# A causal depthwise convolution of 31 taps on VectorE: two alternating sums, with ScalarE making the first taps and all of the small group's products

## The reference

```python
h = xn @ w_in
a, b, q, k, v, ga, gb = jnp.split(h, SPLITS, axis=-1)
glu = a * jax.nn.sigmoid(b)
...
def conv_branch(glu_hist, w_dw, b_dw, conv_ln_g, conv_ln_b, w_conv_out, b_conv_out):
    y = lax.conv_general_dilated(glu_hist, w_dw[:, None, :], window_strides=(1,), padding='VALID',
                                 dimension_numbers=('NWC', 'WIO', 'NWC'),
                                 feature_group_count=D_CONV) + b_dw
    y = jax.nn.silu(layernorm(y, conv_ln_g, conv_ln_b))
    return y @ w_conv_out + b_conv_out
```

## Time and profile before

| what | value |
|---|---|
| median of 3 runs (lowest, highest) | 1535.66 us (1534.71, 1536.74) |
| profiled execution, its own time | 1535.57 us |
| its span, first to last instruction | 1532.7 us |
| mean granted TensorE clock | 0.942 of full speed |
| busy over the span: PE, DVE, ACT, POOL | 86%, 74%, 41%, 18% |
| prompt taps, line 1108 | 240 instructions, 307.7 us busy |
| sample taps, line 1111 | 240 instructions, 66.6 us busy |

### The profile page before, as it was taken

How to read it: one execution, slowest core, us unless ns; L and a number is a source line. 1 busy time by engine, 2 the same in 40 slices (tenths; PEclk the granted TensorE clock), 3 DMA queues, 4 the chain that set the end, 5 groups by cost and what they waited for, 6 DMA issues and landing times. The chain is left out here.

```text
span 1532.7 us, 25464 instructions
## 1 busy us (share of the span) xinstructions
PE 1312.5 (86%) x8761; PEld 780.9 (51%) x8761; DVE 1140.4 (74%) x1553; ACT 631.9 (41%) x903; POOL 276.6 (18%) x276
## 2 busy tenths in 40 slices
PE   2589999976999998997978987888992999888885
PEld 2246666665666664664645554554552555443442
DVE  5437878886599999999998564543655899787783
ACT  5325565654211111111103262332311788767772
POOL 0027001000000000000000000000024476532333
PEclk9999999987799999998988999999995999999997
DMA  6520000022112221221222005427566889999962
GB/s 234 143 56 9 0 0 0 0 104 66 35 43 78 73 60 50 63 64 62 56 60 71 15 30 185 170 86 282 175 245 215 296 319 364 348 320 333 340 231 32
DMA packets 51055, 203.50 MB, mean 133 GB/s; under 512 B 14464, under 2 KB 15552, under 8 KB 38400
## 3 DMA queue, kind: packets, MB, share of 16 engines
q1 hardware_dynamic: 32032, 156.92, 28.1%
q0 software_dynamic: 16656, 36.84, 9.1%
q10 hardware_dynamic: 2304, 8.95, 1.9%
HBM read 180.92 MB, written 39.72 MB: 144 GB/s over the span
## 5 line engine op out<-in xcount | busy, mean ns | idle before, releaser
L1108 DVE SCALAR_TENSOR_TENSOR big<-c_region,c_taps,big 128x1024 f32 (+1 forms) x240 | 307.7, 1282 | 0.0
L72 PE MATMUL c_psb<-xnT,w_taken 128*128 128x364 f16 x456 | 146.4, 321 | 2.3 <-DVE f_w_l L1003 2.3
L73 PE MATMUL c_psb<-xnT,w_taken 128*128 128x364 f16 x456 | 146.2, 321 | 0.0
L74 PE MATMUL c_psb<-xnT,f_w_l 128*128 128x364 f16 x456 | 146.1, 320 | 0.0
L72 PE MATMUL c_psa<-xnT,w_taken 128*128 128x364 f16 x312 | 100.9, 323 | 17.3 <-DVE c_gate_b L1009 17.3
L72 PE MATMUL o_psH<-e_gu,big 128*128 128x512 f16 x256 | 100.9, 394 | 1.6 <-issue 1.5
L73 PE MATMUL o_psH<-e_gu,big 128*128 128x512 f16 x256 | 101.5, 397 | 0.0
L74 PE MATMUL o_psH<-e_gu,big 128*128 128x512 f16 x256 | 101.3, 396 | 0.0
L73 PE MATMUL c_psa<-xnT,w_taken 128*128 128x364 f16 x312 | 100.6, 323 | 0.0
L74 PE MATMUL c_psa<-xnT,f_w_l 128*128 128x364 f16 x312 | 100.6, 322 | 0.0
L2089 DVE SCALAR_TENSOR_TENSOR e_gu<-e_gu 128x2048 f16<-128x2048 f32 x34 | 77.8, 2290 | 19.7 <-ACT e_gu L1861 19.7
(11 more groups left out here) (338 smaller groups left out, 3382.1 us busy)
## 6 DMA issues: line engine op xcount, KB each, us to landing
e_gu<-w_gu SPq DMA_DIRECT2D x34, 1024.0 KB, 25.5
w_taken<-w_feat SPq DMA_DIRECT2D x48, 512.0 KB, 5.3
e_d<-w_dn SPq DMA_DIRECT2D x17, 1024.0 KB
xnT<-w_gu SPq DMA_DIRECT2D x14, 1024.0 KB, 35.9
big<-w_gu SPq DMA_DIRECT2D x14, 1024.0 KB, 33.1
m_gates<-gates POOLq DMA_DIRECT2D x8, 1092.0 KB, 5.8
xnT<-w_dn SPq DMA_DIRECT2D x7, 1024.0 KB
big<-w_dn SPq DMA_DIRECT2D x7, 1024.0 KB
```

The costliest lines, as they stand in the source:

```text
L72: pe.matmul(out, stat[0], mov[0], start=start, stop=False)
L73: pe.matmul(out, stat[0], mov[1], start=False, stop=False)
L74: return pe.matmul(out, stat[1], mov[0], start=False, stop=stop)
L1108: dve.scalar_tensor_tensor(y_p, glu[:, p, j:j + SEQ], tap, y_p, op0=ALU.mult, op1=ALU.add).then_inc(tap_done, 1)
```

## The change

`conv` keeps two sums for the prompt. Even taps add to `y`, odd ones to a new row `y_odd`, both rows of 1,024 columns of float32. Tap 0 with the bias and tap 1 are now made by ScalarE (`first_taps`), VectorE does taps 2 to 30 and adds the two rows at the end. For the sample group ScalarE makes all 31 products (`sample_taps`), 31 instructions of 64 columns, into `prods`, laid out as 31 blocks of 64 columns; VectorE adds them in one `tensor_reduce` whose inner axis steps 64 floats (256 bytes) from product to product. `y_odd` and `prods` lie in the area `caT`, which the first chunk's sample attention uses earlier and the layer norm later. Each tap now waits for the tap before the last one. The two inner calls of `low` move from after taps 11 and 20 to after taps 12 and 22 (19 and 27 in the first chunk), and `sample_norm` and `sample_out` of the first chunk move from after taps 5 and 11 to after 13 and 20.

```diff
+        y_odd = room32[:, 0:SEQ]
+        prods = room32[:, SEQ:SEQ + TAPS * TS].rearrange("p (j n) -> p j n", j=TAPS)
...
-        NTAP = 2 * TAPS
+        NTAP = TAPS
+        even_done, odd_done, prod_done, taps_go = sem("c_even"), sem("c_odd"), sem("c_prod"), sem("c_taps_go")
...
+            def first_taps(k, p):
+                act.wait_ge(glu_done, 2 * k + 1)
+                act.wait_ge(even_done, k)
+                act.sem_inc(taps_go, 1)
+                act.activation(row(y, k)[:, 0:SEQ], glu[:, p, 0:SEQ], ACT.Identity,
+                               scale=taps[:, ds(k, 1), 0:1].rearrange("p a b -> p (a b)"),
+                               bias=vecs[:, 0, ds(k, 1)]).then_inc(even_done, 1)
+                act.wait_ge(tap_done, NTAP * k)
+                act.sem_inc(taps_go, 1)
+                act.activation(y_odd, glu[:, p, 1:1 + SEQ], ACT.Copy,
+                               scale=taps[:, ds(k, 1), 1:2].rearrange("p a b -> p (a b)")).then_inc(odd_done, 1)
+
+            def sample_taps(k, p):
+                act.wait_ge(glu_done, 2 * k + 2)
+                act.sem_inc(taps_go, 1)
+                seqs = glu[:, p, HIST + SEQ:].rearrange("p (b n) -> p b n", b=NSEQ)
+                for j in range(TAPS):
+                    out = prods[:, j].rearrange("p (b i) -> p b i", b=NSEQ)
+                    tap = taps[:, ds(k, 1), j:j + 1].rearrange("p a b -> p (a b)")
+                    if j == 0:
+                        act.activation(out, seqs[:, :, 0:DSEQ], ACT.Identity, scale=tap,
+                                       bias=vecs[:, 0, ds(k, 1)]).then_inc(prod_done, 1)
+                    else:
+                        act.activation(out, seqs[:, :, j:j + DSEQ], ACT.Copy, scale=tap).then_inc(prod_done, 1)
...
                 cut(4 * k + 4, 0)
+                first_taps(k, p)
                 cut(4 * k + 5, 1)
...
                 gate_a_leaves(k)
                 cut(4 * k + 6, 2)
+                sample_taps(k, p)
...
                 dve.wait_ge(glu_done, 2 * k + 2)
+                dve.wait_ge(even_done, k + 1)
+                dve.wait_ge(odd_done, k + 1)
+                for j in range(2, TAPS):
                     tap = taps[:, ds(k, 1), j:j + 1].rearrange("p a b -> p (a b)")
-                    dve.wait_ge(tap_done, NTAP * k + 2 * j - 1)
-                    dve.scalar_tensor_tensor(y_p, glu[:, p, j:j + SEQ], tap, y_p, op0=ALU.mult,
+                    y_j = y_odd if j % 2 else y_p
+                    if j > 3:
+                        dve.wait_ge(tap_done, NTAP * k + j - 3)
+                    dve.scalar_tensor_tensor(y_j, glu[:, p, j:j + SEQ], tap, y_j, op0=ALU.mult,
                                              op1=ALU.add).then_inc(tap_done, 1)
...
+                dve.wait_ge(prod_done, TAPS * k + TAPS)
+                dve.tensor_reduce(y_s, prods.rearrange("p j n -> p n j"), AX.X, ALU.add).then_inc(tap_done, 1)
+                dve.wait_ge(tap_done, NTAP * k + TAPS - 2)
+                dve.tensor_tensor(y_p, y_p, y_odd, ALU.add).then_inc(tap_done, 1)
```

More of the change, by code:

```diff
@@ L928, in chunk @@
                     sample_new_probs()
+                    act.wait_ge(taps_ld, 16)
+                    act.wait_ge(vec_ld, 16)
                 cut(4 * k + 4, 0)
+                first_taps(k, p)
                 cut(4 * k + 5, 1)
@@ L1098, in conv @@
                 y_p = row(y, k)[:, 0:SEQ]
-                y_s = row(y, k)[:, SEQ:T].rearrange("p (b i) -> p b i", b=NSEQ)
+                y_s = row(y, k)[:, SEQ:T]
                 dve.wait_ge(glu_done, 2 * k + 2)
[L1101 to L1104, removed]
@@ L1105, in conv @@
-                for j in range(1, TAPS):
+                dve.wait_ge(even_done, k + 1)
+                dve.wait_ge(odd_done, k + 1)
+                for j in range(2, TAPS):
                     tap = taps[:, ds(k, 1), j:j + 1].rearrange("p a b -> p (a b)")
-                    dve.wait_ge(tap_done, NTAP * k + 2 * j - 1)
-                    dve.scalar_tensor_tensor(y_p, glu[:, p, j:j + SEQ], tap, y_p, op0=ALU.mult,
+                    y_j = y_odd if j % 2 else y_p
+                    if j > 3:
+                        dve.wait_ge(tap_done, NTAP * k + j - 3)
+                    dve.scalar_tensor_tensor(y_j, glu[:, p, j:j + SEQ], tap, y_j, op0=ALU.mult,
@@ L1109, in conv @@
                                              op1=ALU.add).then_inc(tap_done, 1)
[L1110 to L1113, removed]
+                    if first and j == 13:
                         sample_norm()
-                    if first and j == 11:
+                    if j == (19 if first else 12):
+                        low(4 * k + 6, 2)
@@ L1116, in conv @@
+                    if first and j == 20:
                         sample_out()
-                    if j == 11:
-                        low(4 * k + 6, 2)
                     if j == 18 and p == 1:
                         gated(u)
-                    if j == 20:
+                    if j == (27 if first else 22):
                         low(4 * k + 7, 3)
+                dve.wait_ge(prod_done, TAPS * k + TAPS)
+                dve.tensor_reduce(y_s, prods.rearrange("p j n -> p n j"), AX.X, ALU.add).then_inc(tap_done, 1)
```

## The result

| | kernel before | changed kernel |
|---|---|---|
| median (lowest to highest) | 1535.6 us (1534.7 to 1536.7) | 1518.4 us (1513.4 to 1521.5) |
| the profiled execution: time, span | 1535.6, 1532.7 us | 1521.5, 1519.0 us |
| ratio, 95% interval | | 0.9882 (0.9867 to 0.9897) |

The change takes 17 us off, 1.2%. Lines from 850 on have other numbers in the changed kernel: `glu` is L1048, `low` L1035, `gated` L1041, `cut` L856.

A forecast was written before the change was run, and what follows sets the result against it. VectorE's queue was taken to bound the kernel from chunk 1's start to the last tap. Gains of 9.6 us in the loop, 0.6 in chunk 1 and 5.4 at the turns sum to 15.6: 1520 us, range 1509 to 1531 (about 0.8).

The forecast's parts named there:

- VectorE sets the end, and what it saves from chunk 1 on comes off the total: From chunk 1's start to the last tap, VectorE's queue alone sets the end; seven chunks count, chunk 0's saving is lost.
- 29 long taps at 1.21 us: VectorE's remaining long taps in each chunk's convolution start 1.21 us apart, 35.1 us in all.
- The alternation itself gains nothing: Two sums bring no gain by themselves, since each long tap already had a short one between it and its predecessor.
- The reduce 3.6 us: VectorE's addition of the sample's products per chunk: 1,984 floats at 1.75 ns over 150 ns, 3.5 us after overlap.
- both bounds: Limits for the reduce: 2.2 us at the adjacent-element rate, 5.8 us at line 1991's whole duration per element.
- Rival 2: The reduce costs as with adjacent elements, 2.2 instead of 3.6 us, 9.8 us more gained: 1510 us; chance 0.11.
- Rivals 3 and 4: Dearer reduce: 2.1 to 2.9 ns per element, 1525 to 1535 us, chance 0.15; or beyond that, over 1539 us, 0.06.
- The new stall: VectorE waits 2.4 us per chunk before its second `low`, because ScalarE's second `cut` stands behind `first_taps`.
- The loop's turn: VectorE's gap from branch to next step falls from 2.9 to 0.2 us with the shorter body, twice: 5.4 us gained.
- ScalarE's products are free: ScalarE's 31 products, about 8 us per chunk, delay nobody; VectorE asks for them 35 us later.
- rival 5: ScalarE's small products take 1 us each and hold up `gate_b_leaves` by 15 us: about 1536 us; chance 0.03.
- `gated` 27.7 us after `glu`: In a chunk on VectorE, `gated` starts 27.7 us after `glu` instead of 31.3, so TensorE's stalls shrink.

## Why the prediction was right

Forecast 1520 us, measured 1518.4; forecast 15.6 us less in the stage, measured 17.3.

- **VectorE sets the end, and what it saves from chunk 1 on comes off the total.** Right. The 17.3 us of the stage reach the layer norm and the whole stretch to the experts' start as 16.5 us less (the 0.9 us between being chunk 1's later start), and the median fell by 17.2. That these two agree so closely is in part luck, since the experts' loop alone took 316.5 us in one profile of the changed kernel and 312.4 in the other. Chunk 0's savings were lost: VectorE ended 9.91 us before ScalarE's copy of `a`, against 3.02 before, and chunk 1 started no earlier.
- **29 long taps at 1.21 us.** They start 1.195 us apart. This is the term that was mis-sized most: 29 x 0.015 x 7 = 3 us more gained. Part of it is hidden in the total by the turn (4.9 us, forecast 5.4) and the stall (17.1 us, forecast 16.8). I had taken the distance from a long tap to a short one in the loop; in chunk 1 of the kernel before it is 1.19 to 1.20 (469.64 to 470.83, for one).
- **"The alternation itself gains nothing".** Wrong as stated. The reason given, that the short taps had covered the dependence, is right, and it is what the kernel with one sum shows: without them the second sum is worth 38.8 us. But in the loop even a chain with short taps between lost 0.04 us a pair, some 29 x 0.04 x 6 = 7 us, which the kernel with the sample's taps back, with its two sums and its separate semaphore, does not lose. The time forecast did not suffer, since its sum set 29 x 1.21 us against the 43.8 us measured in a loop's chunk, which had that loss in it.
- **The reduce 3.6 us, from line 1991's 1.75 ns an element.** It took 3.47 to 3.57. The nearest row of the same kind of walk beat both bounds. Rival 2 (2.2 us) needed adjacent floats; the kernel that has them shows just that, 2.21. Rivals 3 and 4 (a step eight times as long is dearer) are ruled out. In the Trainium skill, on the page "Vector Engine (DVE) Microarchitecture Reference", section "Measured stream behaviour on trn2", 1.73 ns stands for one of two sources hopping 4 KiB at every element, and 2.50 for both sources, or the destination, stepping 24 words. The reduce, which has one source, took 1.71 with its step of 64 words; that is near the first, and the 5.1 us that the prediction estimated from the second did not come.
- **The new stall, 2.4 us.** 2.49 to 2.51 in the loop, 2.13 in chunk 1. The chain (`glu`, hand-over, two first taps, `cut`, hand-over) stands in ScalarE's timeline in the order in which it was added up, and turning two calls round removes it. Its parts differ a little: the prediction put a hand-over at 0.1 us and named rows that don't show one. In chunk 1 the two took 0.14 and 0.04 us, in the loop 0.34 (from 513.57 to 513.91) and 0.21, while ScalarE's three steps overlapped twice by 0.1. The prediction's two variants, 2.2 with overlapping steps and 2.6 where register steps show, both came: the first in chunk 1, the second in the loop.
- **The loop's turn, 5.4 us from the body's length.** The idle time before `glu` behind a turn was 3.35 and 3.27 us and is now 0.89 and 0.84: 4.9 us measured. A turn took 0.4 us, not the 0.2 of the attention's loop. That the length brings the gap is shown; for the short body the place didn't matter, where it was moved.
- **ScalarE's products are free.** 31 in 7.7 us, ready 25 us early; rival 5 is out. In chunk 4 branch B's gate leaves right behind them, without a wait for TensorE, and still costs nothing: TensorE waits in the loop only for `gated`. Even at 397 ns each they did not show.
- **`gated` 27.7 us after `glu`.** 588.15 - 560.55 = 27.6. TensorE's stalls in the convolution shrank from 26.7 to 9.6 us. `mean(7)` started at 805.59 (forecast 806), chunk 1 at 463.2 (462).

By chunks: a chunk of the loop gained 1.86 us (chunk 2; forecast 1.6), chunk 1 1.2 us (0.6), the turns 4.9 (5.4): 6 x 1.86 + 1.2 + 4.9 = 17.3 us, the stage's 17.3.

What the prediction did not weigh is how near the kernel stood to a better one. The change removes 4 us of VectorE's work in a chunk and gives 2.5 back at once to a wait that two lines in another order shorten to 0.6.

## What to carry to other kernels

When work is handed to an idle engine, look at what the busy engine needs next from that engine's queue: here two taps that would have cost VectorE 1.38 us were moved to ScalarE, in front of a step that VectorE was about to wait for, and cost 2.5; behind that step they cost 0.6. A chain of dependent instructions on VectorE needs either other work between its steps or a second accumulator, as far as these runs show, and taking the filler out without adding the accumulator made this kernel slower than it had been. For a reduce over products that another engine writes, let the writer take the long step and the reader the adjacent floats; and count a loop body's instructions before trusting that its turn is free.

## What was unexpected of the hardware

- The same dependent VectorE instructions were slower inside this kernel's loop than written out: dependent taps of 1,024 columns are 1.32 us apart outside it and 1.44 in it; with a 64-column instruction between them, 1.395 and 1.43. With two independent chains the distance is 1.195 in both.
- ScalarE's 64-column products with a step of 31 floats on the output took 397 ns a record against 339, but followed each other at the same 0.25 us.
- One-float memsets on VectorE have records of 59 ns but follow each other every 28 ns (106 in 3.02 us).
